# Loading four expert matrices, tokens, norms and router between the first two output-projection weights, and forming the router logits with the tokens stationary

## The reference

```
u = rms_norm(h);  proj = u @ w_in                     # q, k, v twice, out-gate, gates A and B
y_a = differential_attention(...) @ w_branch_attn
y_d = gated_deltanet(...) @ w_branch_dn
mixed = sigmoid(gate_a) * y_a + sigmoid(gate_d) * y_d
h = h + mixed @ w_out
x = rms_norm(h)                                        # norm2_w
group = argmax(softmax(x @ router_group_w + b))        # 1 of 4 groups
top 2 of the 8 experts of that group, by x @ router_expert_w + b
h = h + sum of the chosen experts: (silu(x @ w_gate[e]) * (x @ w_up[e])) @ w_down[e]
out = rms_norm(h)[16:]
```

## Time and profile before

| | us |
|---|---|
| median of 3 runs | 690.97 (690.14 to 691.37) |
| profiled execution | 685.91 |
| its span | 684.1 |
| PE busy | 614.6 (90%) |
| DVE busy | 338.8 (50%) |
| ACT busy | 267.0 (39%) |

### The profile page before, as it was taken

The page is one execution under the profiler, slowest core; times in us unless marked ns, Lnnn a source line. Parts: engine busy times, 40 slices in busy tenths (PEclk is TensorE's granted clock), DMA queues, the critical chain, the costliest instruction groups (busy, mean ns, idle before and its releaser), DMA issues.

```text
span 684.1 us, 14436 instructions
## 1 busy us (share of the span) xinstructions
PE 614.6 (90%) x5923; PEld 510.8 (75%) x5923; DVE 338.8 (50%) x744; ACT 267.0 (39%) x594; POOL 42.8 (6%) x92
## 2 busy tenths in 40 slices
PE   8999999999999998999899799999888856849864
PEld 7999998889988888999799799987444524425341
DVE  5443449999868658465755378624211101101102
ACT  6355458667686444235332946313101000101003
POOL 8300000000000001100310100000000000000000
PEclk9999999999999999999999999999999979788989
DMA  9945453232333331221321158899999999999992
GB/s 291 325 144 185 145 164 96 91 124 80 107 124 124 124 123 64 64 73 52 95 93 63 62 173 273 360 422 421 396 421 419 421 421 422 422 422 422 421 396 81
DMA packets 71297, 156.05 MB, mean 228 GB/s; under 512 B 7234, under 2 KB 56500, under 8 KB 59460
## 3 DMA queue, kind: packets, MB, share of 16 engines
q1 hardware_dynamic: 70048, 155.06, 60.7%
q10 hardware_dynamic: 1188, 0.12, 0.2%
HBM read 154.12 MB, written 1.05 MB: 227 GB/s over the span
## 4 chain that ended last, share of the span: by engine, by line
PE 61%; DVE 15%; DMA 14%; issue 4%; ACT 4%; ACTq 0%; DVEq 0%
PE bank L817 28%; DMA arena<-in_expert_w_down_dram 11%; PE bank L1244 5%; PE bank L1222 5%; PE bank L998 5%; DMA arena<-in_expert_w_gate_dram 4%; DVE w_lo L307 4%; PE bank L802 3%; DVE arena L1809 3%; PE bank L976 2%; PE bank L1207 2%; PE bank L941 2%; PE bank L1254 2%; DVE arena L1848 1%; ACT w_hi L302 1%
## 5 line engine op out<-in xcount | busy, mean ns | idle before, releaser
L817 PE MATMUL bank<-uT_hi,w_hi 128*128 128x272 f32 (+1 forms) x568 | 171.9, 303 | 5.6 <-DVE w_lo L307 3.9
L817 PE MATMUL bank<-uT_hi,w_lo 128*128 128x272 f32 (+1 forms) x568 | 162.5, 286 | 0.0
L817 PE MATMUL bank<-uT_lo,w_hi 128*128 128x272 f32 (+1 forms) x568 | 162.4, 286 | 0.0
L307 DVE TENSOR_TENSOR w_lo<-arena,w_hi 128x1024 fp32r<-128x1024 f32 x88 | 108.7, 1237 | 53.6 <-ACT w_hi L302 53.2
L817 PEld LDWEIGHTS bank<-uT_hi,w_hi 128*128 128x128 f32 x568 | 107.6, 190 | 10.2 <-issue 8.4
L817 PEld LDWEIGHTS bank<-uT_lo,w_hi 128*128 128x128 f32 x568 | 107.9, 190 | 1.4 <-issue 0.5
L817 PEld LDWEIGHTS bank<-uT_hi,w_lo 128*128 128x128 f32 x568 | 107.8, 190 | 0.0
L302 ACT ACTIVATE w_hi<-arena 128x1024 fp32r<-128x1024 f32 x88 | 92.2, 1052 | 0.5 <-DMA arena<-in_w_in_dram 0.4
L1244 PE MATMUL bank<-arena 128*32 128x512 f32 x256 | 39.8, 775 | 28.3 <-DMA arena<-in_expert_w_down_dram 25.9
L1222 PE MATMUL bank<-arena 128*32 128x256 f32 x1024 | 59.0, 390 | 5.3 <-DMA arena<-in_expert_w_gate_dram 5.3
L1222 PEld LDWEIGHTS bank<-arena 128*32 128x32 f32 x1024 | 33.5, 113 | 28.0 <-issue 7.0
(11 more groups left out here) (346 smaller groups left out, 1023.6 us busy)
## 6 DMA issues: line engine op xcount, KB each, us to landing
arena<-in_w_in_dram SPq DMA_DIRECT2D x36, 1024.0 KB, 5.2
arena<-in_expert_w_gate_dram SPq DMA_DIRECT2D x32, 1024.0 KB, 21.2
arena<-in_expert_w_up_dram SPq DMA_DIRECT2D x32, 1024.0 KB, 23.2
arena<-in_expert_w_down_dram SPq DMA_DIRECT2D x28, 1024.0 KB, 20.1
arena<-in_w_branch_attn_dram SPq DMA_DIRECT2D x4, 1024.0 KB, 5.3
arena<-in_w_branch_dn_dram SPq DMA_DIRECT2D x4, 1024.0 KB, 5.1
arena<-in_w_out_dram SPq DMA_DIRECT2D x4, 1024.0 KB, 5.4
arena<-in_expert_w_down_dram SPq DMA_DIRECT2D x8, 512.0 KB, 15.6
```

What stands on the lines that cost most here:

```text
L307: nc.vector.tensor_tensor(w_lo[q % NSPLIT], src, w_hi[q % NSPLIT].bitcast(F32), ALU.subtract).then_inc(w_lo_ready, 1)
L817: last = pe.matmul(ps[:, 0:b.shape[2]], a[:, c, :], b[:, c, :], start=(c == 0 and i == 0), stop=(c == NC - 1 and i == 2))
```

## The change

Two edits. The first moves issues on SP: at out-unit 0 SP now waits for tile 79, and issues twins 4 and 5, the tokens, and (after `yd_lo_ready`) the norms and the router; then out-unit 1, twin 8, slot 11 of batch 0 (after all 24 gates are multiplied), and then out-units 2 and 3. The second forms the logits with 128 tokens as the stationary operand and 36 router columns moving, in `bank[6]` and `bank[7]` for the two token blocks, so that they come out upright; the copy to `lgT` and the turning back are gone; after the last output tile the turn of the last columns comes first, then the logits of pieces 2 and 3, and then the seeds. ACT's scaling of the tokens waits for `logits_ready` instead of `lgT_ps`.

```diff
-                if u == N_UNITS - 2:
+                if u == N_UNITS - 4:

                     sp.wait_ge(tile_ready, FIRST["gb"] + 8)
+                    for twin in (4, 5):
+                        load_unit(EPB, True, twin)
                     for t in range(TT):
                         sp.dma_start(h_tok[:, t, :], x[0, t * P:(t + 1) * P, :]).then_inc(h_in, 16)
-
-            sp.wait_ge(yd_lo_ready, 2)
-            sp.dma_start(norm2_pc, ...)
...
+                    sp.wait_ge(yd_lo_ready, 2)
+                    sp.dma_start(norm2_pc, ...)
+                    sp.dma_start(fnorm_b, ...)
+                    sp.dma_start(r_w[:, :, 0:4], ...)
+                    sp.dma_start(r_w[:, :, 4:36], ...)
+                    sp.dma_start(r_b[:, 0:4], ...)
+                    sp.dma_start(r_b[:, 4:36], ...)
+                if u == N_UNITS - 3:
+
+                    load_unit(EPB, True, NC)
+                    sp.wait_ge(gate_ready, 3 * H)
+                    load_unit(0, False, SLOTS - 1)
...
-            for s in (0, 1, 4, 5):
+            for s in (0, 1):
                 load_unit(EPB, True, s)
             for i, s in enumerate(out_slots):
...
-                if i == 1:
-                    load_unit(EPB, True, NC)
...
                 for c in (2 * i, 2 * i + 1):
-                    last = pe.matmul(bank[6][0:36, 0:SEQ], r_w[:, c, :], u2T[:, c, :], start=(c == 0), stop=(c == NC - 1))
+                    for t in range(TT):
+                        last = pe.matmul(bank[6 + t][:, 0:36], u2T[:, c, t * P:(t + 1) * P], r_w[:, c, :],
+                                         start=(c == 0), stop=(c == NC - 1))
                 if i == 3:
-                    last.then_inc(lgT_ps, 1)
+                    last.then_inc(logits_ready, 1)
...
-                    piece_logits(j // 2 - 1)
+                    if j < 7:
+                        piece_logits(j // 2 - 1)
                     piece_seed(1, j // 2 - 1)
             piece_turn(3)
+            piece_logits(2)
+            piece_logits(3)
             piece_seed(1, 3)
             piece_seed(0, 0)
-            piece_logits(3)
-            pe.wait_ge(lgT_ready, 1)
-            for t in range(TT):
-                last = pe.transpose(bank[6][:, 256 + 64 * t:256 + 64 * t + 36], lgT[0:36, t * P:(t + 1) * P], ident[0:36, 0:36])
-            last.then_inc(logits_ready, 1)
...
-            act.wait_ge(lgT_ps, 1)
+            act.wait_ge(logits_ready, 1)
...
-            dve.wait_ge(lgT_ps, 1)
-            dve.tensor_copy(lgT[0:36, :], bank[6][0:36, 0:SEQ]).then_inc(lgT_ready, 1)
```

More of the change, by code:

```diff
@@ L196, in hybrid_block @@
         r_b, norm2_pc = at(u2_start + TT * D + UNIT, 36), at(u2_start + TT * D + UNIT + 36, NC)
-        lgT = new(SEQ)
         ssq_part = new(TT, 4)
@@ L258, in hybrid_block @@
             sem(n) for n in ("ssq2_ready", "var2_ready", "rstd2_ready", "u2_ready", "hT_ps", "hT_ready"))
-        lgT_ps, lgT_ready, f_u2T_ps, f_u2T = sem("lgT_ps"), sem("lgT_ready"), sem("f_u2T_ps"), sem("f_u2T")
+        f_u2T_ps, f_u2T = sem("f_u2T_ps"), sem("f_u2T")
         logits_ready, r_exp_in, r_exp, assigned, ranked, routed = (sem("logits_ready"), sem("r_exp_in"), sem("r_exp"), sem("assigned"), sem("ranked"), sem("routed"))
@@ L476, in _, with load_unit @@
             sp.dma_start(xin[0:META, 2, :], meta_tokens).then_inc(x_in[2], 16)
+            def load_unit(first_expert, odd, s):
+                signal = (twin_in if odd and s in TWINS else slot_in)[s]
+                if s < NC:
+                    e, m = divmod(s, 2)
+                    src = (w_gate_e, w_up_e)[m]
+                    dst = pair_of(e, odd)[:, m, :]
+                else:
+                    e = s - NC
+                    src, dst = w_down_r, down_in(e, odd)
+                sp.dma_start(dst, src[:, bass.ds(first_expert + e, 1), :].rearrange("p a x -> p (a x)")).then_inc(signal, 16)
             for t in range(TT):
@@ new lines, in _ @@
+                    sp.dma_start(norm2_pc, norm2_w[0].rearrange("(p c) -> p c", c=NC)).then_inc(norms_in, 16)
+                    sp.dma_start(fnorm_b, final_norm_w.unsqueeze(0).broadcast_to([P, D])).then_inc(norms_in, 16)
+                    sp.dma_start(r_w[:, :, 0:4], router_group_w[0].rearrange("(c p) n -> p c n", p=P)).then_inc(norms_in, 16)
+                    sp.dma_start(r_w[:, :, 4:36], router_expert_w[0].rearrange("(c p) n -> p c n", p=P)).then_inc(norms_in, 16)
+                    sp.dma_start(r_b[:, 0:4], row(router_group_b, 4)).then_inc(norms_in, 16)
@@ L525, in wait_tiles @@
+                    sp.dma_start(r_b[:, 4:36], row(router_expert_b, 32)).then_inc(norms_in, 16)
+                if u == N_UNITS - 3:
+                    load_unit(EPB, True, NC)
+                    sp.wait_ge(gate_ready, 3 * H)
+                    load_unit(0, False, SLOTS - 1)
             def wait_tiles(s):
@@ L538, in _ @@
             for s in range(SLOTS):
-                if s not in out_slots and s not in OUT_HI:
+                if s not in out_slots and s not in OUT_HI and s != SLOTS - 1:
                     wait_tiles(s)
@@ L2077, in _ @@
             for t in range(TT):
-                mark(stt(lg[:, t, :], bank[6][:, 256 + 64 * t:256 + 64 * t + 36], rstd[:, t:t + 1], r_b, ALU.mult, ALU.add))
+                mark(stt(lg[:, t, :], bank[6 + t][:, 0:36], rstd[:, t:t + 1], r_b, ALU.mult, ALU.add))
             follow()
```

## The result

The changed kernel took 697.28 us (median of 8 runs, 692.72 to 699.58), the one before 690.34 (8 runs beside them). The ratio is 1.0088, interval 1.0061 to 1.0115: 4.2 to 7.9 us slower, 6.1 in the middle. Forecast were 696.0 and +5.0. In a later comparison the ratio was 1.0111 (1.0073 to 1.0149).

The account below looks back on a forecast made before the run. The prediction took PE's finish of batch 0 to set the end, with expert transfers gapless afterwards. 5.4 + 1.6 - 1.5 - 0.5 = +5.0 us moved the median from 690.97 to 696.0, range 690.5 to 700.5.

Parts of the forecast that it names:

- The end follows PE at batch 0: The end moves with PE finishing batch 0; a microsecond of delay on output tiles or routing is one at the end.
- The four matrices' return: Expert queue after 430: four matrices less to read give back 0.5 us, bounds 0 to 1.0.
- The delay of out-unit 3: At block 7's low part: `w_out` queued behind the moved loads makes it 5.4 us later, bounds 3.6 to 7.9.
- SP can issue all this in time: On SP's queue: longest issue 3.18 us, with 14 us before the first out-unit's turn, so issuing adds no delay.
- The clock: After PE's standstill in tile 88: one stretch at half clock costs 1.6 us, bounds 0 and 3.2.
- The logits: Routing up to the ranking product: 1.3 us of waits and turning back plus 0.2 from products, gain 1.5, bounds 0 and 1.8.
- rival C: Delay 3.6, no slow clock, logits -1.8, batch 0's down products at full clock -1.7: about 0, 691; chance 10%.
- A: Expert queue the limit from 430 on: four matrices less end 10 us earlier, 681, or 684 to 687; chance 5%.
- B: `w_out` lands in time, out-unit 3 by 428, so the logits alone make it faster: 689.0; chance 8%.
- D: Router over 3 us of service holds up out-units, delay 7.9, clock falls twice, 3.2: +9.6, 700.6; chance 15%.
- three signs of being wrong: Out-unit 3 landing before 429, PE not stopping in tile 88, or several matrices queued after batch 0's down products.

Follow-up runs that it names:

- again: The changed kernel unaltered, measured once more in a later comparison with the kernel before: ratio 1.0111.
- e2: The changed kernel with the logits formed as before, so only the moved issues remain: 1.0126 of the kernel before.
- e4: The changed kernel with the router's two matrices and biases issued behind out-unit 3: 1.0050 of the kernel before.
- e13: The changed kernel with the router's four loads issued by GpSimd instead of SP: 1.0045 of the kernel before.
- e6: The changed kernel with 24 unread products ahead of block 6 and 8 ahead of block 7 of tile 88: 1.0104, in a second run 1.0087, of the kernel before.
- e1: The changed kernel with SP's issues as before, so only the new logits remain: 0.9977 of the kernel before.
- e5: The changed kernel with the four expert matrices back in their old places; tokens, norms and router stay early: 0.9970 of the kernel before.
- e10: As e9, with the four expert matrices back in their old places: 1.0000 of the kernel before.
- e9: As e3, with the router's four loads issued by GpSimd instead of SP: 685.20 us, 0.9943 of the kernel before.
- e3: The changed kernel with all that was moved ahead of out-units 1 to 3 issued right behind out-unit 3 instead: 0.9971 of the kernel before.
- e7: The kernel before with 12 more idle PE products ahead of the ranking product: 1.0020 of the kernel before.

## Why the prediction was right, and where its sizes were off

**The end follows PE at batch 0: right in this direction.** In the slower kernels with PE's delay (changed, again, e2, e4, e13, e6 twice) the down load is 4.8 to 10.9 us later than before, 3.3 in e4, and the last gate matrix 3.4 to 10.2 later, each within 1.3 us of its own. But I had written that a microsecond is a microsecond, without a limit. The other way it holds for less than one: e1, e5 and e10 give PE 2.2 to 3.9 us, and 0.2 to 0.4 arrive at the last gate matrix of their traces (their timed runs gained 1.6, 2.1 and 0.0). The two limits stood within a microsecond of each other before the change, which the 6.9 and 6.7 us to landing did show.

**The four matrices' return, 0.5 us.** It can't be read from the runs of the changed kernel alone; its queue was empty at batch 0, as forecast, so that at most the 2.1 us that were queued at 476.12 before could come back. In a kernel where PE isn't late they are worth 2.7 (e9 against e10).

**The delay of out-unit 3, forecast 5.4: measured 8.8**, the low part of block 7 ending 29.9 us after the mark against 21.1. That `w_out` comes late behind what was moved ahead of it was right, and this is the term that was mis-sized. Up to the norms the queue's sum held, 11.7 us from twin 4's issue against 12.0. From there, 421.3, to out-unit 1 at 428.8 it took 7.5 us against 5.0. The step that failed is "SP can issue all this in time". The router's larger matrix landed 1.7 us after the norms, within the 2.2 that I gave the router; but SP was held at the bias until 422.01, the engines ran nearly dry, and out-unit 1, issued at 422.65, needed 6.2 us, not much more than a load into an empty queue. The stretch of before from which I priced the router, 419 to 423 at a share of 0.33, already showed it: I took 1.3 us of service from it and left out that it lasted 4 us. SP was held then as well (columns as in the earlier trace rows):

```profile
417.58 3.02 SPq L509 DMA_DIRECT2D arena<-in_router_group_b_dram  x1
```

From out-unit 1 to out-unit 3 it took 12.1 against 10.6. There the engines were busy (share 1.06, 385 GB/s from 428.8 to 440.9). These are 4.7 MB, and the four loads that I counted have 4.2: at least 0.4 MB of later loads, over 1 us, went in between, and my sum served them strictly in order. e4 agrees: its low part of block 7 is 4.6 us late, and my sum without the router gives 3.2. e5 shows that without the matrices it all fits.

**The clock, forecast 1.6: measured 2.1** (e6). The fall came as the trace of before had it after a wait of 3.90. The Trainium skill (TensorE: Matmul & The Clock Gate, Part 1) says that the number of slow products differs from run to run. By that the loss could have failed to come; in the five traces where PE stood idle in the stop (changed, again, e2, e4, e13) it always came, with 8.4 to 9.0 us for the 51 products that take 6.22 at full clock; in that its size did differ from trace to trace.

**The logits, forecast 1.5: measured 2.16** at the ranking (e1, e3, e5). The 1.3 us of waits went as worked out. The rest was the products: eight instructions of 36 columns in 0.82 us where four of 256 took 0.98, and the seed behind them 0.51 instead of 0.63, twice between the tiles (0.6 in all); the remaining 0.3 came behind the last tile. At the ranking the sum is 8.8 + 2.1 - 2.2 = +8.8 (rounded terms), and the trace has 64.17 - 55.37 = 8.80.

**From there to the end** batch 0's clock fall of before was missing, -1.7, which I had named in rival C only; it isn't a part of the change, for it was there in e9 and e10 and missing in e7. The last gap in the queue then lies at the up matrices, 8.7 us later than before, less the 0.9 us queued there before: +7.8, with 8.3 and 7.0 in the two traces. The runs say 4.2 to 7.9. The delay and the clock together were 3.9 us larger than I had them, the logits and batch 0's clock gave 2.4 us more: that the two cancel in good part is luck, and the forecast of +5.0 is better than its working.

**The rivals.** A and B are out: the matrices alone didn't help, and `w_out` came late. C needed a delay of 3.6; it was 8.8. D's delay of 7.9 was nearer than mine. Its condition, a router of over 3 us of service, isn't shown for the changed kernel, where the small pieces held up SP more than the engines; in e13 the router costs 3.1 against e4. D's time of 700.6 didn't come since the clock fell once, and the logits gave more. What I looked for in the trace came in kind, later and larger than listed. With the 3.0 us of the mark taken off, out-unit 1 was issued at 419.7 and not near 417, and out-unit 3 landed at 438.0 and not near 434; PE stood still for 8.1 us and not 4 to 6, and the ranking came 8.8 later and not 4 to 6. The down load went out at 494.6 and landed after 7.1 us. None of the three signs of being wrong was there.

## What to carry to other kernels

A transfer that is moved ahead because "the DMA engines are idle there" stands in one queue with what comes behind it; add up the bytes and the small pieces between the new place and the next consumer, and compare with the time at which that consumer asks. Look also at how long each issue holds the engine that issues, for the DMA engines can run dry behind it. Where two limits lie within a microsecond, a gain on one of them alone gives little, as the traces of e1 and e10 show, and both together give what each seemed to promise (e9). Put many tiny pieces on the queue of an engine with nothing to do, or behind what is needed first.

## What the runs showed of the hardware that was not expected

- The router's two matrices and biases, 0.17 MB in pieces of 16 and 128 B, cost out-unit 3 about 4 us issued by SP (changed against e4) and 3.1 issued by GpSimd (e13 against e4), where as many bytes of expert matrices take 0.4.
- An issue on SP can be held for long by what was issued ahead of it, 8.14 us for a bias of 2 KB, and meanwhile the DMA engines ran nearly dry: share 0.20 and 30 GB/s from 422 to 425. The same four loads on GpSimd took it 1.12, 0.90, 0.56 and 0.55 us:

```profile
412.39 1.12 POOL L744 DMA_DIRECT2D arena<-in_router_group_w_dram  x1 [14.64 <-PE bank L823]
413.52 0.90 POOL L745 DMA_DIRECT2D arena<-in_router_expert_w_dram  x1
414.41 0.56 POOL L746 DMA_DIRECT2D arena<-in_router_group_b_dram  x1
414.96 0.55 POOL L747 DMA_DIRECT2D arena<-in_router_expert_b_dram  x1
```

- PE's clock falls at places that change from one execution to the next without any change there; a fall in batch 0's down products costs 1.6 to 1.7 us. Two such falls put the profiled execution of the changed kernel 3.0 us behind before it reached the change, and batch 0's down products took 3.64 us in nine traces and 5.2 to 5.3 in five.
